# First layer's joined attention maps turned by 16-bit DMA in three head groups, with the second group's product two units later

## The chip, the cores and the metric

The kernel runs on one core of one Trainium2 chip. The metric is the device time of one execution in microseconds. The core has TensorE (PE in the rows; PEld is its weight load), VectorE (DVE), ScalarE (ACT), GpSimd (POOL) and SyncE (SP, which here only issues DMAs). Each engine runs its own list of instructions in order, and semaphores are all that orders one engine against another.

## The reference, cut to what matters

Four transformer layers over 256 tokens of width 1024, all in float32. The first layer's mixer is a differential attention with eight heads, two maps per head, with an ALiBi penalty:

```python
s = jnp.einsum('mbhqd,mbhkd->mbhqk', q, k) * scale + bias    # two maps m = 0, 1 for every head
a = jax.nn.softmax(s, axis=-1)
a = a[0] - lam * a[1]                                       # the joined map
o = jnp.einsum('bhqk,bhkd->bhqd', a, v)                     # 128 columns of v per head
o = rmsnorm(o, subln) * (1.0 - lam_init)
mix = o.reshape(B, S, D_MODEL) @ w_o
```

Each layer goes on with `h = h + mix`, a gated feed-forward block of width 2816, and a gated side input. Layers 2 to 4 have other mixers: neighbourhood, stick-breaking and forgetting attention, 16 heads each.

## The kernel before, in words

**Tiling.** The 256 tokens are T = 2 tiles of 128 query rows. Weights stream from HBM in units of 128x1024 floats through a ring of six buffers. For each unit SyncE loads `raw`, ScalarE writes a rounded copy `whi` (L828), VectorE writes the remainder `wlo` (L1138), and TensorE multiplies in three passes (hi hi, hi lo, lo hi). A layer has 108 units. In the first layer's attention the units 0 to 23 are the QKV projection: four head groups `j` of two heads each, six units per group (four for Q and K, two for V; the V units of two neighbouring groups are shared out over both). Units 24 to 31 are the output projection.

**Order.** Nothing is scheduled at run time. The steps of attention are hung between the units by tables written by hand, `PE_STEPS`, `ACT_STEPS` and `DVE_STEPS`: group `j` has row `r` at unit `6j + 4 + r`. A step stands in front of the engine's work for that unit, or behind it (`+`, or `*` for the groups before the last). ScalarE's work for unit `s` is the split of unit `s+4`, VectorE's the split of unit `s+3`. If two groups have steps at one unit, the later group's come first. The function `steps` (L160) also moves the product steps: `V_WAITS` (L147) gives rows 8, 9 and 10 for `pv0`, `pv1` and `turno`, always behind, and takes the place of the table's rows wherever the line at L172 says so. In the first layer that is for groups 0 and 2. Group 1 keeps the table's rows: `pv0` in front at row 6, `pv1` behind at row 7, `turno` behind at row 8. Group 3, the last, has an order of its own (`last_steps`).

**The steps of a group in the first layer**, tile by tile (0 and 1):
- `evacqk`: Q and K leave PSUM (for groups 1 to 3 VectorE's L1393); `turnqk`: ScalarE's L899 rounds them and VectorE's L1342 writes the remainder `qklo` (named split_qg in the rows).
- `scores0`, `scores1`: TensorE L1818, after both remainders are there; VectorE L1235 takes them from PSUM into `z` with the bias added. Both tiles use the same PSUM banks.
- `exp0`, `exp1`: ScalarE L934.
- `post0`, `post1`: VectorE L1276 to L1282 divides by the sums and joins two maps to one, so that 128x512 floats per tile are left in `z`.
- `turnp0`, `turnp1`: TensorE L1765 transposes the four 128x128 blocks of `z` against the identity into PSUM, and ScalarE L961 copies them to `aT`.
- `pv0`, `pv1`: TensorE L1847 multiplies the turned map by V. ScalarE L966 squares the result for its norm, GpSimd L672 and L673 make `r_o`, the root's inverse, and VectorE L1379 writes the scaled result to `o`.
- `turno`: TensorE L1765 transposes `o`, ScalarE L972 and VectorE L1158 split it into `ohi` and `olo` for the output projection.

**GpSimd** builds the bias of group 3 (`alibi(3)`) and constant tables of later layers (`later_tables`) right after it has made `r_o` of group 1, tile 1. Only then does it come to `r_o` of group 2.

**The other way to turn a map** is there already, for groups 0 to 2 of the second and third layer. VectorE writes the low and the high 16-bit halves of `z` as two planes into the bias tile of the group, which has been used up (`split_p`, L1253); SyncE issues one transposing DMA into `aT` (L553, in `turn_p`); ScalarE puts the halves together again in the bias tile (`join`, L944); the product reads that tile. SyncE waits for the planes of VectorE's step at unit `s-9` just before it loads unit `s`, a load that waits for VectorE's split of the same step.

Of the kernel before, what the change touches and what calls it, by code (L numbers as in the profile page):

```python
# [24 lines left out]
U16 = mybir.dt.uint16  # L25
# [5 lines left out]
P = 128  # L31
S = 256
# [7 lines left out]
HG = 4  # L40
L_DA, L_NA, L_SB, L_FX = range(4)
# [62 lines left out]
def count(labels):  # L104
# [16 lines left out]
    L_FX: [["evacqk"], [], ["turnqk0", "turnqk1/"], ["scores0"], ["scores1"], ["turnp0"], ["turnp1"], ["pvt*"]],  # L121
}
ACT_STEPS = {
    L_DA: [["evacqk"], ["turnqk"], [], ["exp0"], ["exp1"], ["turnp0"], ["pv0", "turnp1"], ["pv1*"], ["turno*"]],
    L_NA: [["evacqk"], ["turnqk"], [], ["exp0"], ["exp1"], ["turnp0"], ["turnp1"], ["pvt*"], ["join0"], ["join1"]],
    L_SB: [["evacqk"], ["turnqk"], [], ["exp0"], ["exp1"], ["turnp0"], ["turnp1"], ["pvt*"], ["join0"], ["join1"]],
    L_FX: [["evacqk"], [], ["turnqk0", "turnqk1+"], [], ["exp0", "exp1+"], ["turnp0"], ["turnp1"], ["pvt*"]],
# [13 lines left out]
def joined(L):  # L141

    return L in (L_NA, L_SB)
# [16 lines left out]
def steps(tables, L, s, place="front"):  # L160

    found = []

    for j in (range(HG) if L == L_FX and s == GROUP_UNITS + QK_UNITS else range(HG)[::-1]):
        r = s - GROUP_UNITS * j - QK_UNITS
        if L == L_FX and j == 0 and r > 0:
            r = r if r == 1 else r - 1 if r > 2 else -1
        if 0 <= r < len(tables[L]) + 3:
            names = tables[L][r] if r < len(tables[L]) else []
            if L == L_DA and j == HG - 1 and r >= LAST_PV:  # L170
                names = last_steps(tables)[r - LAST_PV]
            if j % 2 == 0 or (L == L_FX or joined(L)) and j < HG - 1:  # L172
                names = [x for x in names if x.rstrip("+*") not in V_WAITS[L]]
                names = names + [x + "+" for x in V_WAITS[L] if V_WAITS[L][x] == r]
            for name in names:
                late = name.endswith("+") or name.endswith("*") and j < HG - 1
                if place == ("middle" if name.endswith("/") else "behind" if late else "front"):
                    found.append((name.rstrip("+*/"), j))
    return found


def keys(L, t):
    return P if L >= L_SB and t == 0 else S
# [26 lines left out]

def by_dma(L, j):

    return L in (L_NA, L_SB) and j < HG - 1


P_TURN = count([(L, j, t) for L in range(LAYERS) for j in range(HG) for t in range(T) if by_dma(L, j)])
# [53 lines left out]
EV = {x: n for n, x in enumerate(EV_LIST)}  # L270
# [41 lines left out]
def build(nc, a, out):  # L312
    ctx = ExitStack()
    with ctx:
# [12 lines left out]
        h = sb("h", [P, T, D])  # L327
# [14 lines left out]
        aT, gain = aT_gain[:, 0:T * 1024].rearrange("p (t c) -> p t c", t=T), aT_gain[:, T * 1024:T * 1024 + GAIN_ROWS]  # L342
        bias = sb("bias", [P, T, HG, 1024])
# [52 lines left out]
        tb = [ps(f"turn{b}", [P, 512]) for b in range(2)]  # L396
# [53 lines left out]
        def wait_out(eng, e):  # L450

            eng.wait_ge(turn_out[e % 2], e // 2 + 1)

        def p_source(L, j, t):

            return bias[:, t, j, :].bitcast(U16)[:, 0:8 * keys(L, t)]

        def p_target(L, t):

            return aT[:, t, :].bitcast(U16)[:, 0:8 * keys(L, t)]  # L460

        def p_halves(tile, L, t, h):

            return tile.bitcast(U16).rearrange("p (x c h) -> p x c h", c=S, h=2)[:, :, 0:keys(L, t), h]

        def scores_wait(eng, L, j, t):

# [341 lines left out]
        def _(act):  # L809
# [52 lines left out]
            def attention(L, name, j):  # L862
                t = int(name[-1]) if name[-1] in "01" else 0
# [56 lines left out]
                elif name.startswith("exp"):  # L920
                    if L == L_SB:
                        scores_wait(act, L, j, t)
                        if j and by_dma(L, j - 1):
                            act.wait_ge(p_joined, P_TURN[(L, j - 1, t)])
                        tmp = aT[:, t, :].rearrange("p (x c) -> p x c", c=S)[:, :, 0:kk]
                        act.activation(tmp, zt, ACT.Sigmoid, scale=-1.0)
                        act.activation(zt, zt, ACT.Sigmoid).then_inc(sp_ready, 1)
                    else:
                        if L == L_FX:
                            act.wait_ge(mx_ready, 2 * j + t + 1)  # L930
                        else:
                            scores_wait(act, L, j, t)
                        for x in range(4):
                            ins = act.activation(zt[:, x, :], zt[:, x, :], ACT.Exp, bias=mx[:, t, x:x + 1],  # L934
                                                 scale=-1.0, accum_out=sums[:, t, x:x + 1])
                        ins.then_inc(e_ready, 1)
                elif name.startswith("join"):
                    if not by_dma(L, j):
                        return
                    n = P_TURN[(L, j, t)]  # L940
                    act.wait_ge(p_turned[t], 16 * ((n - 1) // T + 1))
                    for h in range(2):
                        c = 4 * kk
                        ins = act.activation(p_halves(bias[:, t, j, :], L, t, h),  # L944
                                             p_target(L, t)[:, h * c:(h + 1) * c].rearrange("p (x c) -> p x c", c=kk),
                                             ACT.Copy)
                    ins.then_inc(p_joined, 1)
                elif name.startswith("turnp"):
                    if by_dma(L, j):
                        return  # L950
                    e = EV[("p", L, j, t, 0)]
                    act.wait_ge(turned, e + 1)
                    if j and by_dma(L, j - 1):
                        act.wait_ge(p_joined, P_TURN[(L, j - 1, t)])
                    dst = aT[:, t, 0:512]
                    if kk == P:
                        dst = aT[:, t, :].rearrange("p (x k c) -> p x k c", k=2, c=P)[:, :, 0, :]
                        act.activation(dst, tb[e % 2][:, :].rearrange("p (x c) -> p x c", c=P), ACT.Copy)\
                            .then_inc(turn_out[e % 2], 1)
                    else:  # L960
                        act.activation(dst, tb[e % 2][:, :], ACT.Copy).then_inc(turn_out[e % 2], 1)  # L961
                elif name in ("pv0", "pv1"):
                    e = EV[("pv", L, j, t)]
                    act.wait_ge(turned, e + 1)
                    for x in range(2):
                        ins = act.activation(aT[:, t, x * P:(x + 1) * P], tb[e % 2][:, x * P:(x + 1) * P], ACT.Square,  # L966
                                             accum_out=ss_o[:, t, x:x + 1])
                    ins.then_inc(so_ready, 1)
                elif name in ("turno", "pvt"):
                    e = EV[("o", L, j)]  # L970
                    act.wait_ge(turned, e + 1)
                    act.activation(ohi[:, 2 * j:2 * j + 2, :], tb[e % 2][:, :].rearrange("p (k c) -> p k c", k=2),  # L972
                                   ACT.Copy).then_inc(turn_hi, 1)
# [148 lines left out]
        def _(dve):  # L1122
# [125 lines left out]
            def split_p(L, j, t):  # L1248

                for h in range(2):  # L1250
                    c = 4 * keys(L, t)
                    to = p_source(L, j, t)[:, h * c:(h + 1) * c].rearrange("p (x c) -> p x c", x=4)
                    ins = dve.tensor_copy(to, p_halves(z[:, t, :], L, t, h))  # L1253
                ins.then_inc(p_planes, 1)

            def after_exp(L, j, t):
# [20 lines left out]
                if L == L_DA:  # L1277
                    link(dve.tensor_scalar(lamc[:, t, :], rsum[:, t, 2:4], lam[:, 1:2], None, ALU.mult))
                    for b in range(2):
                        e0, e1 = (z[:, t, q * 512 + b * 256:q * 512 + b * 256 + 256] for q in range(2))  # L1280
                        link(dve.tensor_scalar(e1, e1, lamc[:, t, b:b + 1], None, ALU.mult))
                        ins = dve.scalar_tensor_tensor(out=e0, in0=e0, scalar=rsum[:, t, b:b + 1], in1=e1,  # L1282
                                                       op0=ALU.mult, op1=ALU.add)
                    ins.then_inc(a_ready, 1)
                    return
                zt = z[:, t, :].rearrange("p (x c) -> p x c", c=S)[:, :, 0:kk]
                dve.tensor_tensor(zt, zt, rsum[:, t, :].unsqueeze(2).to_broadcast([P, 4, kk]), ALU.mult)\
# [305 lines left out]
        def _(pe):  # L1593
# [182 lines left out]
            def attention(L, name, j):  # L1776
# [62 lines left out]
                elif name in ("pv0", "pv1"):  # L1839
                    e = EV[("pv", L, j, t)]  # L1840
                    use(e)
                    wait_out(pe, EV[("p", L, j, t, 0)])
                    for kt in range(T):
                        pe.wait_ge(bank_out[2 + kt], outs(2 + kt, L, j) + 1)
                    for n, (q, b, k) in enumerate(p_blocks(L, t)):
                        c = b * P
                        ins = pe.matmul(tb[e % 2][:, c:c + P], aT[:, t, n * P:(n + 1) * P],  # L1847
                                        qkv[:, B, k, 512 + c:512 + c + P], start=(k == 0), stop=(k == T - 1))
                    ins.then_inc(turned, 1)
                elif name == "pvt":  # L1850
# [194 lines left out]
```

## Time and profile before

| | |
|---|---|
| median of 3 runs | 1318.11 us (1317.69 to 1318.17) |
| profiled execution | 1318.08 us, of which the span is 1316.0 us |
| TensorE busy | 1300.7 us (99%), 6642 matmuls |
| VectorE busy | 965.8 us (73%) |
| ScalarE busy | 847.4 us (64%) |
| GpSimd busy | 127.5 us (10%) |
| share of the chain that ended last | PE 88%, DVE 7%, ACT 2% |
| granted TensorE clock | 1.000 (2.4 GHz) |

The profile is of one execution; its times are counted from the start of the span. The first layer's attention lies from 0 to about 125 us. Busy shares are means over the whole span, so the stretches have to be read one by one. In a timeline a row is a start, a duration, the engine, the line, the operation, `out<-in`, the size, and how many such instructions the row merges; a bracket at its end tells how long the engine had been idle and who released it. Instructions of one engine overlap a little: the next one starts some hundredths before the last one's end, and with matmuls a tenth or more.

### The profile page before, as it was taken

What the parts mean: (1) busy time and instruction counts of PE and PEld (TensorE: products, weight loads), DVE (VectorE), ACT (ScalarE), POOL (GpSimd) and SP (SyncE); (2) the same over time, 40 slices, a digit from 0 to 9 for tenths busy, and PEclk for the clock granted to TensorE, in tenths of its full rate; (3) what the DMA queues carried; (4) which work ended last, traced back from release to release, by engine and by line L of the source; (5) the groups of instructions that cost most, each with busy time, mean ns of one, the idle gap of its engine ahead of it and who ended that gap; (6) DMA issues with size and microseconds to landing.
All of it is one profiled execution on the core that took longest, in us unless ns stands there. A gap on an engine that the chain in (4) does not pass through costs nothing.

```text
span 1316.0 us, 20045 instructions
## 1 busy us (share of the span) xinstructions
PE 1300.7 (99%) x6642; PEld 1082.7 (82%) x6642; DVE 965.8 (73%) x1669; ACT 847.4 (64%) x1459; POOL 127.5 (10%) x179
## 2 busy tenths in 40 slices
PE   9999999999999999999999999999999999999998
PEld 7987888888898788888888878888887778888887
DVE  7887677777799666666699976666677887666664
ACT  7666666656778666665677666666578766666654
POOL 6031244310000000000010000000002210000000
PEclk9999999999999999999999999999999999999999
DMA  9444688876496466667647656666645535666661
GB/s 335 145 156 136 200 247 243 241 241 176 177 232 195 147 196 207 207 207 213 214 145 198 179 172 197 207 206 211 211 165 183 176 131 163 200 208 209 210 225 48
DMA packets 205056, 255.28 MB, mean 194 GB/s; under 512 B 72962, under 2 KB 163249, under 8 KB 204992
## 3 DMA queue, kind: packets, MB, share of 16 engines
q1 hardware_dynamic: 201984, 245.42, 59.4%
q0 software_dynamic: 2832, 8.49, 2.9%
q8 instruction: 37, 0.61, 0.2%
q10 hardware_dynamic: 176, 0.54, 0.1%
q14 instruction: 27, 0.22, 0.0%
HBM read 238.33 MB, written 1.13 MB: 182 GB/s over the span
## 4 chain that ended last, share of the span: by engine, by line
PE 88%; DVE 7%; ACT 2%; issue 1%; DMA 1%; POOL 0%; SPq 0%; DVEq 0%; ACTq 0%
PE acc L1604 14%; PE acc L1606 13%; PE acc L1605 13%; PE sc L1604 12%; PE sc L1606 12%; PE sc L1605 12%; PE turn L1765 3%; DVE wlo L1138 2%; PE acc L1715 2%; PE acc L1717 2%; PE acc L1716 2%; PE turn L1867 1%; DVE z L1235 1%; PE sc L1818 1%; ACT whi L828 1%
## 5 line engine op out<-in xcount | busy, mean ns | idle before, releaser
L828 ACT ACTIVATE whi<-raw,aT_gain 128x512 fp32r<-128x512 f32 (+2 forms) x612 | 403.8, 720 | 79.5 <-PE sc L1606 53.5
L1138 DVE SCALAR_TENSOR_TENSOR wlo<-raw,aT_gain,whi 128x512 fp32r<-128x512 f32 (+2 forms) x612 | 431.9, 760 | 28.4 <-ACT whi L828 24.2
L1604 PE MATMUL sc<-whi,xhi 128*128 128x512 f32 x640 | 249.4, 390 | 0.0
L1606 PE MATMUL sc<-whi,xlo 128*128 128x512 f32 x640 | 249.0, 389 | 0.0
L1605 PE MATMUL sc<-wlo,xhi 128*128 128x512 f32 x640 | 249.0, 389 | 0.0
L1604 PE MATMUL acc<-whi,xhi 128*128 128x512 f32 x432 | 173.1, 401 | 1.1 <-DVE wlo L1138 0.5
L1606 PE MATMUL acc<-whi,xlo 128*128 128x512 f32 x432 | 168.6, 390 | 0.0
L1605 PE MATMUL acc<-wlo,xhi 128*128 128x512 f32 x432 | 168.4, 390 | 0.0
L828 ACT ACTIVATE whi<-raw 128x1024 fp32r<-128x1024 f32 x120 | 125.9, 1055 | 63.5 <-PE acc L1606 56.9
L1136 DVE TENSOR_TENSOR wlo<-raw,whi 128x1024 fp32r<-128x1024 f32 x120 | 146.5, 1253 | 0.5 <-ACT whi L828 0.5
L1606 PEld LDWEIGHTS sc<-whi,xlo 128*128 128x128 f32 x640 | 120.1, 188 | 25.2
L1604 PEld LDWEIGHTS sc<-whi,xhi 128*128 128x128 f32 x640 | 120.1, 188 | 24.8
L1605 PEld LDWEIGHTS sc<-wlo,xhi 128*128 128x128 f32 x640 | 120.2, 188 | 24.7
L1401 DVE SCALAR_TENSOR_TENSOR aT_gain<-sc,rstd,aT_gain 128x256 f32<-128x256 f32 x80 | 38.7, 483 | 115.0 <-ACT aT_gain L977 115.0
L977 ACT ACTIVATE aT_gain<-sc,rstd 128x256 f32<-128x256 f32 x80 | 38.0, 475 | 127.3 <-PE sc L1606 127.3
L1604 PE MATMUL acc<-whi,split_qg 128*128 128x512 f32 x288 | 112.4, 390 | 0.0
L1606 PE MATMUL acc<-whi,split_qg 128*128 128x512 f32 x288 | 112.1, 389 | 0.0
L1605 PE MATMUL acc<-wlo,split_qg 128*128 128x512 f32 x288 | 112.0, 389 | 0.0
L1604 PEld LDWEIGHTS acc<-whi,xhi 128*128 128x128 f32 x432 | 81.3, 188 | 18.8 <-issue 2.1
L1606 PEld LDWEIGHTS acc<-whi,xlo 128*128 128x128 f32 x432 | 81.1, 188 | 17.5
L1605 PEld LDWEIGHTS acc<-wlo,xhi 128*128 128x128 f32 x432 | 81.4, 189 | 15.1
L672 POOL TENSOR_SCALAR rstd<-ss 128x2 f32<-128x2 f32 x12 | 2.6, 219 | 919.2 <-ACT spare L851 919.2
(212 smaller groups left out, 2068.4 us busy)
## 6 DMA issues: line engine op xcount, KB each, us to landing
raw<-in_ffn_w_gu SPq DMA_DIRECT2D x176, 256.0 KB
raw<-in_qk SPq DMA_DIRECT2D x62, 512.0 KB
raw<-in_ffn_w_gate SPq DMA_DIRECT2D x88, 256.0 KB
raw<-in_ffn_w_up SPq DMA_DIRECT2D x88, 256.0 KB
raw<-in_ffn_w_down SPq DMA_DIRECT2D x44, 512.0 KB
raw<-in_ffn_w_d SPq DMA_DIRECT2D x44, 512.0 KB
raw<-in_ple_w_gate SPq DMA_DIRECT2D x32, 512.0 KB
raw<-in_da_w_qkv SPq DMA_DIRECT2D x8, 512.0 KB
```

The source lines that it names most:

```text
L828: ins = act.activation(whi[:, u % RING, c0:c1], raw[:, u % RING, c0:c1], ACT.Copy, scale=scale)
L977: act.activation(aT[:, 0, t * 256:t * 256 + 256], bank[:, 0:256], ACT.Sigmoid, scale=rs(L, 1, t))\
L1136: ins = dve.tensor_tensor(lo, w, hi.bitcast(F32), ALU.subtract)
L1138: ins = dve.scalar_tensor_tensor(out=lo, in0=w, scalar=gain[:, g:g + 1], in1=hi.bitcast(F32), op0=ALU.mult, op1=ALU.subtract)
L1401: dve.scalar_tensor_tensor(out=sg, in0=banks[t][:, 256:512], scalar=rs(L, 1, t), in1=sg, op0=ALU.mult, op1=ALU.mult).then_inc(gmid, 1)
L1604: pe.matmul(dst, xh, wh, start=first, stop=False)
L1605: pe.matmul(dst, xh, wl, start=False, stop=False)
L1606: return pe.matmul(dst, xl, wh, start=False, stop=last)
L1715: pe.matmul(dst, wh, xh, start=first and k == 0 and c == 0, stop=False)
L1716: pe.matmul(dst, wl, xh, start=False, stop=False)
L1717: ins = pe.matmul(dst, wh, xl, start=False, stop=last and k == 1 and c == 1)
L1765: ins = pe.transpose(tb[e % 2][0:cols, n * rows:(n + 1) * rows], src, ident[0:rows, 0:rows])
```

## The change

Four things are different. First, `by_dma` takes in the first layer, so the maps of its groups 0, 1 and 2 are turned by the DMA instead of TensorE. The helpers get a factor, `p_maps`: two joined maps instead of four, so 128x512 floats per tile, as two planes of 512 16-bit elements. Second, ScalarE gets the steps `join0` and `join1` at rows 7 and 8 of the first layer. Third, the condition in `steps` becomes `j < HG - 1`: group 1 of the first layer now has its product at rows 8 and 9 and its `turno` at row 10, all behind, as the groups 0 and 2 have. For all other layers and groups the condition gives what it gave before. Fourth, TensorE's `pv0` and `pv1` wait for the joined map and read it from the bias tile. Group 3 still has its maps turned by TensorE.

```diff
 ACT_STEPS = {
-    L_DA: [["evacqk"], ["turnqk"], [], ["exp0"], ["exp1"], ["turnp0"], ["pv0", "turnp1"], ["pv1*"], ["turno*"]],
+    L_DA: [["evacqk"], ["turnqk"], [], ["exp0"], ["exp1"], ["turnp0"], ["pv0", "turnp1"], ["pv1*", "join0"],
+           ["turno*", "join1"]],
...
-            if j % 2 == 0 or (L == L_FX or joined(L)) and j < HG - 1:
+            if j < HG - 1:
                 names = [x for x in names if x.rstrip("+*") not in V_WAITS[L]]
...
 def by_dma(L, j):
 
-    return L in (L_NA, L_SB) and j < HG - 1
+    return L in (L_DA, L_NA, L_SB,) and j < HG - 1
...
+        def p_maps(L):
+
+            return 2 if L == L_DA else 4
+
         def p_source(L, j, t):
 
-            return bias[:, t, j, :].bitcast(U16)[:, 0:8 * keys(L, t)]
+            return bias[:, t, j, :].bitcast(U16)[:, 0:2 * p_maps(L) * keys(L, t)]
...
                     ins.then_inc(a_ready, 1)
+                    if by_dma(L, j):
+                        dve.wait_ge(a_ready, 2 * j + t + 1)
+                        split_p(L, j, t)
                     return
...
                 elif name in ("pv0", "pv1"):
                     e = EV[("pv", L, j, t)]
                     use(e)
-                    wait_out(pe, EV[("p", L, j, t, 0)])
+                    if by_dma(L, j):
+                        pe.wait_ge(p_joined, P_TURN[(L, j, t)])
+                    else:
+                        wait_out(pe, EV[("p", L, j, t, 0)])
+                    p_t = bias[:, t, j, :] if by_dma(L, j) else aT[:, t, :]
...
-                        ins = pe.matmul(tb[e % 2][:, c:c + P], aT[:, t, n * P:(n + 1) * P],
+                        ins = pe.matmul(tb[e % 2][:, c:c + P], p_t[:, n * P:(n + 1) * P],
```

`p_target`, `p_halves`, `split_p` and the join take `p_maps(L)` in place of 4 in the same way.

## Rows read from the trace of the kernel before

**Rows 1.** The page, part 1: busy us, share of the span, instructions.
```profile
PE 1300.7 (99%) x6642; PEld 1082.7 (82%) x6642; DVE 965.8 (73%) x1669; ACT 847.4 (64%) x1459; POOL 127.5 (10%) x179
```

**Rows 2.** Table by stretch: length, busy per engine, clock, DMA share, GB/s.
```profile
28.50:50.80 22.30, 22.12 (x171) 20.44 (x170) 21.91 (x61) 13.83 (x34) 1.49 (x4) 1.00 0.60 194
58.53:72.00 13.47, 12.51 (x85) 11.32 (x84) 13.15 (x31) 9.18 (x23) 1.06 (x2) 1.00 0.44 150
77.37:96.42 19.05, 19.05 (x132) 17.04 (x131) 18.77 (x45) 12.74 (x29) 6.37 (x16) 1.00 0.52 172
```

**Rows 3.** Chain of waits: start, us, what; one set of four transposes.
```profile
37.83 0.44 PE turn L1765 x4
```

**Rows 4.** Timeline of TensorE in the first layer.
```profile
46.98 0.39 PE L1818 MATMUL sc<-qkT 64*128 64x256 f32 x2
...
55.73 1.05 PE L1847 MATMUL turn<-qkv,aT_gain 128*128 128x128 f32 x8
...
61.05 0.66 PE L1765 MATMUL turn<-ident,z 128*128 128x128 f32 x4 [0.96 <-DVE z L1282]
...
71.24 1.05 PE L1847 MATMUL turn<-qkv,aT_gain 128*128 128x128 f32 x8
72.22 0.39 PE L1818 MATMUL sc<-qkT 64*128 64x256 f32 x2
...
76.10 0.60 PE L1765 MATMUL turn<-ident,o 128*128 128x128 f32 x4
...
92.71 0.38 PE L1818 MATMUL sc<-qkT 64*128 64x256 f32 x2
```

**Rows 5.** Timeline of VectorE in the first layer.
```profile
44.08 1.43 DVE L1342 TENSOR_TENSOR split_qg<-qkv,qkT 128x256 fp32r<-128x256 f32 x4
...
58.53 0.42 DVE L1379 TENSOR_TENSOR o<-turn,r_o 128x256 f32<-128x256 f32 x1 [1.71 <-POOL r_o L673]
...
60.51 0.48 DVE L1282 SCALAR_TENSOR_TENSOR z<-z,rsum 128x256 f32<-128x256 f32 x1
60.91 1.41 DVE L1138 SCALAR_TENSOR_TENSOR wlo<-raw,aT_gain,whi 128x512 fp32r<-128x512 f32 x2
...
69.32 1.42 DVE L1342 TENSOR_TENSOR split_qg<-qkv,qkT 128x256 fp32r<-128x256 f32 x4
...
77.37 0.69 DVE L1158 TENSOR_TENSOR olo<-turn,ohi 128x512 fp32r<-128x512 f32 x1
...
80.68 0.17 DVE L1276 RECIPROCAL rsum<-sums 128x4 f32<-128x4 f32 x1
...
89.89 1.42 DVE L1342 TENSOR_TENSOR split_qg<-qkv,qkT 128x256 fp32r<-128x256 f32 x4
```

**Rows 6.** Timeline of VectorE in the third layer: planes of a tile of 128x512.
```profile
687.49 0.69 DVE L1269 TENSOR_TENSOR z<-z,aT_gain 128x508 f32<-128x508 f32 x1
688.21 0.76 DVE L1253 COPY bias<-z 128x512 uint16<-128x512 uint16 x2
```

**Rows 7.** Timeline of TensorE in the second layer.
```profile
396.78 0.39 PE L1818 MATMUL sc<-qkT 64*128 64x256 f32 x2 [1.28 <-DVE split_qg L1338]
```

**Rows 8.** Timeline of VectorE in the second layer, just before rows 7.
```profile
395.01 1.67 DVE L1338 SCALAR_TENSOR_TENSOR split_qg<-qkv,lam_in,qkT 128x256 fp32r<-128x256 f32 x4
```

**Rows 9.** The transposing DMAs' line: issue ns min/median/max; then time to landing.
```profile
L553 SPq DMA_TRANSPOSE aT_gain<-bias x12: 1237/1835/3716, 365.0 to 733.2; - x12
...
DMA to landing us min/median/max: 3.3/4.3/6.6
```

**Rows 10.** Timeline of ScalarE in the third layer: the join of a tile of 128x512.
```profile
695.76 1.40 ACT L944 ACTIVATE bias<-aT_gain 128x512 uint16<-128x512 uint16 x2
```

**Rows 11.** Timeline of GpSimd in the first layer: bias of group 3, end of the tables.
```profile
74.09 4.41 POOL L666 TENSOR_SCALAR bias<-nab 128x256 f32<-128x256 f32 x8
...
88.17 0.22 POOL L737 TENSOR_SCALAR_AFFINE_SELECT window<-window 64x48 f32<-64x48 f32 x1
```

**Rows 12.** Timeline of VectorE beside GpSimd's first bias builds.
```profile
19.78 3.16 DVE L1138 SCALAR_TENSOR_TENSOR wlo<-raw,aT_gain,whi 128x512 fp32r<-128x512 f32 x4 [1.22 <-ACT whi L828]
```

## Prediction: what the change does to the time

> **Bound now.** The page's busy times come first: TensorE (PE) is busy 99% of the span and VectorE (DVE) 73% [rows 1]. Read alone, that says a PE cut comes out whole and DVE work is free. The table by stretch says otherwise for the layer that is changed: DVE works 21.91 of 22.30 us from 28.50 on, 13.15 of 13.47 from 58.53, and 18.77 of 19.05 from 77.37 [rows 2]. Between these stretches it waits for r_o, the norm of the product (PE product, ScalarE squares, GpSimd power, then DVE's o). So in this layer DVE has no cover of its own except in those waits.
>
> Units are numbered by PE: group j has its first QK unit at 6j, unit 6j+4+r is its row r in the step tables. scores0 of group j+1 (units 12, 18, 24) needs DVE's qk_lo (L1342) of the unit before. Before the change PE starts these at 46.98, 72.22 and 92.71 [rows 4], and L1342 ends at 44.08+1.43 = 45.51, 69.32+1.42 = 70.74 and 89.89+1.42 = 91.31 [rows 5]: slacks of 1.47, 1.48 and 1.40 us. How thin that is shows in the second layer, which turns by DMA already: there PE sat 1.28 us before scores for qk_lo [rows 7], and started 396.78-(395.01+1.67) = 0.10 us after L1338 ended [rows 8].
>
> **What PE loses.** Six sets of four transposes at 0.44 us each in the chain of waits [rows 3]: 2.64 us. The set of group 1, tile 0, also waited 0.96 us for z [rows 4]; nobody waits there now. Together 3.6 us: what a PE-bound reading gives. The deferral moves two products by two units each; it removes nothing. A product costs 72.22-71.24 = 0.98 us [rows 4].
>
> **What DVE gets.** Per tile, a wait for its own z and two copies of 128x512 16-bit elements. The third layer's tile 0 has exactly this shape: the pair takes 0.76 us and starts 0.03 us after its source ends at 687.49+0.69 [rows 6]. Instructions that don't wait start some 0.08 us before the last one ends (60.51+0.48 against 60.91, [rows 5]); the pair gives that back at its end and loses it at its start. So 0.76+0.03 = 0.79, taken as 0.80 us per tile, 1.6 us per group. Nothing is taken off DVE: the evictions that go were ScalarE's. It cannot be below zero; the upper bound, half again for other strides, is 1.2 per tile.
>
> **The chain, step by step.**
> Group 0: DVE works without a break from post0 to qk_lo of group 1, so L1342 ends at 45.51+1.6 = 47.11, and scores0 of group 1 starts at 47.2 instead of 46.98. PE, 0.88 us early by its two lost sets, would have been there at 46.1; it waits 1.1 us, and the gain is gone: +0.2 against before. DVE's wait for r_o that follows (o starts 58.53-55.73 = 2.80 us after its product, [rows 4, 5]) takes the rest of DVE's delay.
> Group 1: before, from o at 58.53 to the end of L1342 at 70.74 are 12.2 us [rows 5]. Added: 1.6; gone: the o of product 0, 0.42-0.08 = 0.34. So 13.5. The product of tile 1 of group 0 starts at 55.73+0.2 = 55.95, o at 58.75, L1342 ends at 72.2, scores0 of group 2 starts at 72.3. PE would be ready at 72.22+0.2-1.96-0.88-0.96 = 68.6: it sits 3.7 us. It starts the scores when it did before, but with the two products (1.96 us) still to do.
> Group 2: products and scores alternate now: scores0 at 72.3, product 0 after 76.10-72.22 = 3.88, scores1 after 0.98, product 1 after another 3.88, at 81.1; o at 83.9. Only then does DVE come to post0 of group 2, which began at 80.68 before [rows 5]. From there to the end of L1342 at 91.31 were 10.6 us; added are o itself (0.34), the olo of the moved turno (0.69-0.08 = 0.6, [rows 5], which lay ahead of post0 before) and 1.6: 13.2. L1342 ends at 97.0, scores0 of group 3 starts at 97.1 instead of 92.71: **+4.4**. PE would be ready at 72.3+(92.71-72.22)+1.96-0.88 = 93.9 and sits 3.2 us.
> After that nothing gives it back or adds to it: DVE waits for r_o of group 2 again, and the last group keeps its own order and its PE transposes. All later weight loads are paced by units.
>
> **What lies beside.** ScalarE loses six evictions and gets twelve copies, 1.40 us for a pair of this shape [rows 10]; it sat in waits for PE, and its joins lie ahead of splits four units early: no cost, up to 0.7 us if a join delays an exp. SP gets six transposing DMAs; its wait for the planes lies ahead of a load that waits for DVE's split of the same step anyway. Issuing takes it 1.2 to 3.7 us and landing 3.3 to 6.6 [rows 9]; the loads queued behind have some five units until they are split, so nothing. The least time from planes to join is about 5 us (group 2, tile 1: planes at 92, join at 97). Even a landing at 6.6 delays ScalarE by some 1.6 us, which splits four units ahead cover.
> GpSimd: the last bias and the tables start after group 1's product 1, so at 84 instead of 74.09; they took until 88.4 [rows 11], 14.3 us, and end near 98.3. r_o of group 2 is due at about 102.7 and the bias at 98: both in time, by 4 and 10 us. But the bias build (4.41 us) now lies beside post0 and the copies of group 2. Four splits beside GpSimd's first bias took 3.16 us [rows 12], where two pairs at 1.41 less overlaps make 2.74 [rows 5]: 15% more. On 4.2 us of DVE that is at most 0.6; zero if these forms are not touched; I take 0.2.
> The Trainium skill has a rule for this (SBUF — State Buffer, SBUF: two separate sides): VectorE and GpSimd share a port pair that one of them holds for a whole instruction while the other blocks. The slower splits agree with it.
>
> **Sum.** 4.4+0.2 = +4.6 us on the profiled run's 1318.08 (span 1316.0 and 2.1 around it), which stands within 0.1 of the median 1318.11: 1322.7 us, a span of 1320.6. The copies at 1.2 per tile would add 0.8 in group 1's chain and 0.8 in group 2's, and GpSimd 0.4 more than taken: up to 1324.7. If the two waits for r_o come out half a microsecond shorter each (2.30 for 2.80): 1321.7.
>
> The Trainium skill says to transpose a full 128x128 block on TensorE if a PSUM destination is acceptable, and by DMA otherwise (VectorE: DVE Perf Modes, Rules for kernel authors). It speaks against this change, for another reason than mine; by that rule alone one would expect a loss here too, and no row tells its size.
>
> **Rivals.**
> 1. **PE keeps what it is relieved of** (faster). It decides if DVE's extra work per group stays under the slack of 1.47 us less what PE comes early, 0.6 us in group 0. [rows 1] speak for it; [rows 2, 6, 7] against. Time: 1318.1-3.6 = 1314.5. Chance 0.10.
> 2. **The first long wait doesn't form** (no change). If group 1's chain were 3.7 us shorter, scores0 of group 2 would start at 68.6, product 1 at 77.4, and group 3's scores at 93.4 instead of 92.71: 1318.8. It needs a DVE that works the stretch from 58.53 with less than its steps take, though it was busy for 13.15 of 13.47 us: chance 0.10.
> 3. **The clock falls.** PE sits 3.7 and 3.2 us, against 0.96 and 1.28 in the waits shown [rows 4, 7], and the granted clock was 1.00 in every stretch of [rows 2]. If it went to the lower of its levels after such a wait, the 3.88 us from scores0 to the next step would take up to twice as long; this is in series with the forecast: +2 to +4 for one fall, 1324.7 to 1326.7. Nothing in the rows shows a fall: chance 0.08.
> The Trainium skill warns of just this: long idle gaps between matmul bursts bring TensorE back to half clock (TensorE: Matmul & The Clock Gate, Why this matters for your kernels).
> 4. **The change doesn't arrive as meant**: the DMA lands so late that joins hold ScalarE, and exp and post with it. If the 1.6 us by which the longest landing of [rows 9] is over the 5 us of group 2 reach DVE's post through one exp: 1324.3. Chance 0.06.
> The forecast has the remaining 0.66.
>
> **Range and chances.** The forecast's own range is 1321.7 to 1324.7. Two in ten outside allow one to leave out rival 1 and most of a fall of the clock, so the range goes from 1318.7 (rival 2, just below) to 1326.2. A measurement of this kernel tells 0.2%, 2.6 us, from no change. Faster by more: rival 1, 0.10. Within: rival 2 and a thin lower edge of the forecast, 0.12. Slower by more: 0.78.
>
> **What would show it.** In the changed kernel's list of waits: PE waits for split_qg L1342 before scores three times, about 1.1, 3.7 and 3.2 us, and no wait for z of group 1. DVE busy over 97% from post0 to L1342 of each group. scores0 of group 3 near 97. In the layers behind, all steps later by the same amount. POOL's tables end near 98. The granted clock 1.00 throughout. Wrong it would be made by waits under 1 us at these places (rival 1 or 2), by PE waiting for the joined planes (rival 4), or by DVE copies far from 0.8 us per tile.

## The result and the profile after

The changed kernel takes 1326.64 us (median; 1325.81 to 1327.69), the kernel before 1318.09 beside it: a ratio of 1.0066 with a 95% interval of 1.0054 to 1.0078, +8.5 us. The forecast was 1322.7 in a range of 1318.7 to 1326.2, so the sign was right and the size was not: +8.5 for +4.6, just over the upper end. The profiled execution is the longest of those shown, 1327.69 us with a span of 1325.9 (+9.9 on 1316.0).

The list of waits of the changed kernel (engine, line, what it waited for: us in total, times, longest). L1826 are the scores, L1350 is qk_lo (L1342 before), L1773 the transposes on PE:

```profile
PE sc L1826 <- DVE split_qg L1350: 8.9, 3, 4.2
...
PE turn L1773 <- DVE z L1287: 1.5, 2, 1.1
```

Three waits, as forecast, and none of PE for a joined plane. The steps of PE around them, from its timeline (start us, us, line, operation, tiles, [idle before, what ended it]); L1859 is the product with the values:

```profile
46.76 0.39 PE L1826 MATMUL sc<-qkT 64*128 64x256 f32 x2 [0.95 <-DVE split_qg L1350]
...
71.87 0.58 PE L1826 MATMUL sc<-qkT 64*128 64x256 f32 x2 [3.67 <-DVE split_qg L1350]
72.22 0.45 PE L1826 MATMUL sc<-split_qg,qkT 64*128 64x256 f32 x2
...
78.28 0.28 PE L1724 MATMUL acc<-xhi,wlo 128*128 128x256 f32 x1
...
78.52 1.05 PE L1859 MATMUL turn<-qkv,bias 128*128 128x128 f32 x8
...
83.37 1.05 PE L1859 MATMUL turn<-qkv,bias 128*128 128x128 f32 x8
100.32 0.58 PE L1826 MATMUL sc<-qkT 64*128 64x256 f32 x2 [4.24 <-DVE split_qg L1350]
...
106.44 1.05 PE L1859 MATMUL turn<-qkv,bias 128*128 128x128 f32 x8
```

Starts in two traces can be compared to some 0.4 us only. The scores of group 0 are ahead of everything that the change touches. The first line here has them in the kernel before, the second in the changed kernel; the third is, in the kernel before, the product that starts at 106.44 above:

```profile
26.68 0.39 PE L1818 MATMUL sc<-qkT 64*128 64x256 f32 x2 [0.26 <-DVE split_qg L1158]
...
26.31 0.38 PE L1826 MATMUL sc<-qkT 64*128 64x256 f32 x2 [0.26 <-DVE split_qg L1163]
...
96.51 1.05 PE L1847 MATMUL turn<-qkv,aT_gain 128*128 128x128 f32 x8
```

Counted from scores0 of group 0, scores0 of group 1 comes after 20.45 us for 20.30 before (+0.15), and scores0 of group 2 after 45.56 for 45.54.

Up to 71.87 this is the forecast: 0.95 for 1.1, 3.67 for 3.7, a start at 71.87 for 72.3. Then comes what it did not have. The product follows 6.65 us after these scores (78.52-71.87) instead of 3.88 [rows 4], and between them one scores matmul takes 0.45 us, where the others show 0.28 to 0.31. The table by stretch, with stretches chosen at such steps (span of the stretch; PE, PEld, DVE, ACT, POOL busy; granted clock; DMA share; GB/s):

```profile
55.00:68.00 13.00, 13.00 (x90) 11.89 (x88) 10.91 (x29) 7.40 (x20) 0.88 (x2) 1.00 0.42 104
71.87:78.00 6.13, 6.13 (x33) 5.91 (x34) 4.02 (x12) 2.94 (x5) 0.00 (x0) 0.50 0.56 173
78.50:99.00 20.50, 17.58 (x130) 16.02 (x128) 15.60 (x36) 12.00 (x36) 9.63 (x23) 0.99 0.40 101
100.32:105.50 5.18, 5.18 (x21) 4.18 (x22) 4.98 (x12) 2.58 (x4) 0.00 (x0) 0.50 0.60 199
106.50:120.00 13.50, 12.32 (x73) 9.96 (x71) 8.72 (x25) 9.37 (x29) 1.79 (x4) 1.00 0.32 99
```

After each of the two long waits the granted clock was 0.50, the lower of its two levels (1.2 GHz for 2.4), for the next 6.2 and 5.2 us, in which PE worked without a break. The Trainium skill names this (TensorE: Matmul & The Clock Gate, Why this matters for your kernels): long idle gaps between bursts of matmuls bring the engine back to half clock. The trace agrees for these two, at 3.67 and 4.24 us.

A further departure is on DVE. Its steps after the o of group 1 (L1387), with the z operations of post0 (L1286, L1287) and the copies (L1258):

```profile
86.17 0.42 DVE L1387 TENSOR_TENSOR o<-turn,r_o 128x256 f32<-128x256 f32 x1 [1.73 <-POOL r_o L678]
...
86.72 0.40 DVE L1283 TENSOR_SCALAR lamc<-rsum,lam 128x2 f32<-128x2 f32 x1
87.15 0.55 DVE L1286 TENSOR_SCALAR z<-z,lamc 128x256 f32<-128x256 f32 x1
87.74 0.56 DVE L1287 SCALAR_TENSOR_TENSOR z<-z,rsum 128x256 f32<-128x256 f32 x1
...
89.34 1.05 DVE L1258 COPY bias<-z 128x512 uint16<-128x512 uint16 x2
...
92.46 0.23 DVE L1283 TENSOR_SCALAR lamc<-rsum,lam 128x2 f32<-128x2 f32 x1
...
93.11 0.48 DVE L1287 SCALAR_TENSOR_TENSOR z<-z,rsum 128x256 f32<-128x256 f32 x1
93.51 0.35 DVE L1286 TENSOR_SCALAR z<-z,lamc 128x256 f32<-128x256 f32 x1
93.90 0.48 DVE L1287 SCALAR_TENSOR_TENSOR z<-z,rsum 128x256 f32<-128x256 f32 x1
94.42 0.76 DVE L1258 COPY bias<-z 128x512 uint16<-128x512 uint16 x2
```

and GpSimd in the same time:

```profile
86.22 3.88 POOL L671 TENSOR_SCALAR bias<-nab 128x256 f32<-128x256 f32 x8
```

The same operations take 0.40, 0.55, 0.56 and 1.05 us beside the bias build, and 0.23, 0.35, 0.48 and 0.76 six microseconds later. From L1283 to the end of the copies that makes 3.67 us for 2.72, 0.95 more. What lies behind adds nothing: the product of group 2 already starts 9.93 us later than before (106.44 for 96.51), the whole of the 9.9 us between the spans.

### The profile page after: what moved, and what is told of

It reads as the page before. It is cut to its first block, busy times and chain, and to the rows that moved or that the text cites. A ratio compares the mean times of both kernels' runs of the same rounds, so it can differ in the third digit from the quotient of the medians.

```text
span 1325.9 us, 20022 instructions
## 1 busy us (share of the span) xinstructions
PE 1302.6 (98%) x6618; PEld 1084.2 (82%) x6618; DVE 970.8 (73%) x1681; ACT 852.0 (64%) x1465; POOL 126.0 (10%) x179
## 4 chain that ended last, share of the span: by engine, by line
PE 85%; DVE 10%; ACT 2%; issue 1%; DMA 1%; POOL 0%; SPq 0%; DVEq 0%; ACTq 0%
PE acc L1612 13%; PE acc L1614 13%; PE acc L1613 13%; PE sc L1612 12%; PE sc L1614 11%; PE sc L1613 11%; DVE wlo L1143 3%; PE turn L1773 3%; PE acc L1723 2%; PE acc L1724 2%; PE acc L1725 2%; PE turn L1879 1%; DVE z L1240 1%; PE sc L1826 1%; DVE z L1287 1%
```

## The experiments

All times are medians, with the kernel before beside them at 1317.80 to 1318.00. The chain theory says: DVE's work from o to qk_lo of groups 1 and 2 sets when PE gets its next scores; the copies and the moved product lengthen it. The rivals were a fall of the clock and GpSimd's work beside DVE.

**One part alone: the copies.** The kernel before, with this behind post of groups 0 to 2 (nobody reads the copies; PE still transposes):

```
+ if j < HG - 1:
+     dve.wait_ge(a_ready, 2 * j + t + 1)
+     for h in range(2):
+         dve.tensor_copy(<plane h>, <half h of z>)
```

> The kernel before, with VectorE's two 16-bit copies added to each tile of groups 0 to 2 and nothing else: TensorE still turns the maps, the planes are used by nobody. Theory (VectorE's chain to qk_lo decides): each group's 1.6 us eat the slack of 1.4 to 1.5 us before scores; TensorE waits for split_qg before scores three times, each under 1 us, the clock stays at 1.00, and the kernel is 0.7 to 1.2 us slower than before. Rival (the copies are the whole cost): 5 to 8.5 us slower. Rival (the DMA or the deferral is the cost): no change.

Measured 1319.12 us, ratio 1.0011 (1.0001 to 1.0021): +1.3. The size holds, near enough; the place does not. PE waited for z before its transposes, 3.1 us in five waits (2.5 in three before), and not for qk_lo. A likely reason, argued and not tested: while PE transposes it has its own work to put against DVE's 1.6 us a group, and what is over shows at the next thing that it needs from DVE.

**One part alone: the deferral.**

```
-            if j % 2 == 0 or (L == L_FX or joined(L)) and j < HG - 1:
+            if j < HG - 1:
```

> The kernel before, with group 1's two products two units later and turno too, TensorE still turning all maps. Theory: VectorE now reaches post0 of group 2 only after the second product's o, and qk_lo of group 3 ends near 93.6 instead of 91.3 while TensorE wants it at 92.9: 1 us slower than before, clock 1.00, one wait for split_qg of about 0.8 us. Rival (deferral is harmless): no change within 0.2 us. Rival (deferral is most of the loss): 4 us and more.

Measured 1321.69, 1.0029 (1.0017 to 1.0040): +3.8 for an expected +1. PE's waits in that kernel:

```profile
PE turn L1765 <- DVE z L1282: 5.7, 6, 1.6
```

The product that is moved takes its o with it, and that o now stands ahead of post0 of group 2 on DVE. So post0 waits for PE's product, ScalarE's squares and GpSimd's norm, and what PE needs next (here z for its transposes, in the changed kernel qk_lo) comes late. The bias build of GpSimd moves too, since it follows the last r_o of group 1, and lies beside that post0:

```profile
82.55 4.14 POOL L666 TENSOR_SCALAR bias<-nab 128x256 f32<-128x256 f32 x8
...
83.47 0.56 DVE L1281 TENSOR_SCALAR z<-z,lamc 128x256 f32<-128x256 f32 x1
...
85.55 1.68 DVE L1138 SCALAR_TENSOR_TENSOR wlo<-raw,aT_gain,whi 128x512 fp32r<-128x512 f32 x2
```

From L1278 to the end of that pair of splits the trace has 4.19 us, where the same steps of group 1 in the changed kernel without its copies take 3.25: some 0.9 of the 3.8 us are an estimate of GpSimd's part.

**The change without its copies.** The copies of L1258 are left out of the changed kernel, so that what is transposed for groups 0 to 2 is not the map.

> The changed kernel without the twelve copies on VectorE: the DMA turns whatever the bias tiles hold, so the first layer's maps of groups 0 to 2 are wrong, and everything else runs as in the changed kernel. Theory: TensorE waits for split_qg about 0, 2.1 and 2 us before the three scores instead of 0.95, 3.67 and 4.24; the clock stays at 1.00; 1 to 2 us slower than before, 6.5 to 7.5 faster than the changed kernel. Rival (DMA, joins on ScalarE or the port are the cost): within 1.5 us of the changed kernel's 1326.6.

Measured 1320.37, 1.0021 (1.0012 to 1.0031): +2.5, over the 1 to 2 expected with a steady clock. The waits are near the expected ones, 2.10 and 2.54 us. Single runs lie between 1319.04 at a mean clock of 1.000 and 1323.41 at 0.996, so the time goes with the clock. In the profiled run it fell after the shorter of the two waits:

```profile
60.00:80.00 20.00, 17.90 (x124) 16.24 (x123) 15.61 (x44) 13.00 (x32) 0.89 (x2) 0.91 0.58 158
```

So the copies are not a small part. Without them 6.0 of the 8.55 us are gone, and the one run at clock 1.000 is 1.2 us slower than before, just the +3.8 of the deferral less 2.64 us for the six sets of transposes [rows 3]. Alone the copies cost 1.3 us; in the changed kernel, beside the deferral and without PE's transposes, far more.

**Without the fall of the clock.** The changed kernel with dummy matmuls in the long waits of groups 2 and 3 (called filler below):

```
+ if L == L_DA and j >= 2 and t == 0:
+     pe.wait_ge(z_ready, ATT[(L, j, t)] - 1)
+     spin(13)
```

> The changed kernel with 13 idle matmuls of the identity (some 2.9 us) ahead of TensorE's wait for qk_lo in groups 2 and 3, where it waited 3.67 and 4.24 us. They add work to nothing that is late. Theory (the clock fell after those two waits, which cost the rest): the mean granted clock is back at 1.000, the waits for split_qg shrink to about 1 us, and the kernel takes 1322.5 to 1323.5, 3 to 4 us less than the changed kernel. Rival (the clock is not the cause, all of it is the chain): 1326 to 1327 as before.

Measured 1323.29, 1.0042 (1.0025 to 1.0059). What PE then shows, the dummies on L1916:

```profile
68.19 3.06 PE L1916 MATMUL sc<-ident 128*128 128x128 f32 x26
72.03 0.39 PE L1829 MATMUL sc<-qkT 64*128 64x256 f32 x2 [0.77 <-DVE split_qg L1350]
...
97.72 0.39 PE L1829 MATMUL sc<-qkT 64*128 64x256 f32 x2 [1.34 <-DVE split_qg L1350]
```

The scores start at 72.03 as without them (71.87), the next matmuls take 0.31 us, and the granted clock is 1.00 where it was 0.50:

```profile
72.03:78.00 5.97, 5.97 (x57) 5.58 (x58) 3.94 (x12) 3.97 (x11) 0.21 (x2) 1.00 0.65 208
97.72:103.00 5.28, 5.28 (x40) 4.53 (x42) 4.98 (x12) 3.03 (x8) 0.00 (x0) 1.00 0.59 186
```

PE does dozens of small matmuls more, 26 in this wait alone, and the kernel is 3.35 us faster (1326.64-1323.29; 3.1 if each is taken against the kernel before beside it). That is what the clock took.

**Where the chain decides, and from where on.** Only groups 0 and 2 turned by DMA, group 1 as before, with no deferral:

> The changed kernel with group 1 as before the change: its maps are turned by TensorE and its product stands at rows 6 and 7. Groups 0 and 2 are turned by DMA. Theory: the copies of group 0 cost the 0.95 us wait and no more; group 1 runs as before; qk_lo of group 3 ends near 92.7, 1.2 us after TensorE could use it. 1318.0 to 1318.8, clock 1.00, the losses of the full change (8.5 us) nearly all gone. Rival (each group's DMA turn costs its share): two thirds of the loss, 1323 to 1324.

Measured 1317.85, 1.0002 (0.9992 to 1.0011). PE has lost four sets of transposes, 1.76 us by [rows 3], and waits for qk_lo instead, 2.0 us in two waits (0.93 and 1.05). By the medians that is an even trade, a little below the expected 1318.0 to 1318.8.

**The deferral halved.** Group 1's products one unit later instead of two:

> The changed kernel with group 1's products and turno one unit later than before instead of two (rows 7, 8 and 9, behind). VectorE then meets the second product's o before scores1 of group 2 and not after it, so post0 of group 2 isn't behind a wait. Theory: the wait before scores0 of group 2 is 2.7 us instead of 3.67, scores0 of group 3 comes near 95.3 with the clock up instead of 97.7 (kernel filler); 2.5 us from the chain and 1.3 to 3 from clock falls: 1322 to 1324, at least 2 us below the changed kernel. Rival (where the product stands doesn't matter, only the copies do): 1326 to 1327.

Measured 1321.84, 1.0037 (1.0022 to 1.0052), and again with the clock: 1320.60 and 1320.71 at 1.000, 1321.84 and 1321.87 at 0.998, 1326.03 at 0.994. One kernel, 5.4 us apart. The wait of group 1 is another one than expected. The product now stands ahead of scores0 of group 2, and PE sat 3.08 us before it. The profile names no releaser, but ScalarE's join (L950) of this map ended at 71.45, 0.1 us before:

```profile
70.07 1.38 ACT L950 ACTIVATE bias<-aT_gain 128x512 uint16<-128x512 uint16 x2
...
71.55 1.13 PE L1860 MATMUL turn<-qkv,bias 128*128 128x128 f32 x8 [3.08 <-issue]
```

The join stood behind ScalarE's rounding of Q and K, which waited for DVE's L1402, so DVE is in this chain too. Qk_lo itself was there at 72.05, and the scores started at 72.61. In this run the clock held through the wait of 3.08 us:

```profile
71.50:77.00 5.50, 5.45 (x49) 5.23 (x50) 4.45 (x15) 4.22 (x10) 0.88 (x2) 1.00 0.61 191
```

**The copies twice**, with the dummies of filler:

> The kernel filler with every copy done twice (the second pair goes to an unused part of the bias tile): 0.68 us more of VectorE per tile, 1.36 per group. Theory (no slack is left in any of the three chains): all of it comes out, 3 x 1.36 = 4.1 us more than filler, 1327.4; where the waits now outlast the idle matmuls by 2 us the clock may fall and add up to 3. Rival (VectorE's waits for r_o take part of it): less than 2 us more, 1325 at most.

Measured 1330.07, 1.0096 (1.0079 to 1.0113): 6.8 us over filler. Counted from scores0 of group 0 (26.13 here, 26.46 in filler), scores0 of the groups 1, 2 and 3 comes 1.33, 2.67 and 4.16 us later than in filler: each of the three chains grew by what was added to it, as expected. The rest is the clock: the last wait grew to 2.83 us in spite of the dummies ahead of it, from 100 to 120 the granted clock was 0.83, against 1.00 in filler, and the product came 6.63 us after scores0 of group 3 for 3.76.

**GpSimd's share, first try.** Filler with the last bias built after group 0's product, at 59, instead of after group 1's:

> The kernel filler with GpSimd's bias build for group 3 right after group 0's product instead of group 1's, so it no longer runs beside post0 and the copies of group 2. Theory (the port they share slowed these, 2.1 us for post0's four passes by the changed kernel's rows where before had them faster): the four passes and the copies are back at their durations, scores0 of group 3 comes 0.8 to 1.0 us earlier, and the kernel takes 1322.3 to 1322.6. Rival (the slower rows are not GpSimd's): the same 1323.3 as filler.

Measured 1324.23, 1.0045 (1.0028 to 1.0061), no gain. The bias build had found the other chain, that from the o of group 0:

```profile
60.02 0.56 DVE L1287 TENSOR_SCALAR z<-z,lamc 128x256 f32<-128x256 f32 x1
60.61 0.56 DVE L1288 SCALAR_TENSOR_TENSOR z<-z,rsum 128x256 f32<-128x256 f32 x1
```

From scores0 of group 1 to that of group 2 this kernel takes 26.07 us, filler 25.12; from there to group 3 24.71, filler 25.69. What was won in group 2 was lost in group 1.

**GpSimd's share, second try.** The bias where DVE has slack of its own:

```
+ if t == 0 and j == 0:
+     pool.wait_ge(unit_done, 12)
+     alibi(3)
```

> The kernel of the run filler (the changed kernel with spinning matmuls before the long waits) with one edit: GpSimd builds the last bias right after unit 12 has begun, at about 47, where VectorE waits 1.46 us for r_o a little later and so has slack of its own. No part of the chains from o to qk_lo of groups 1 and 2 then lies beside GpSimd's bias. My theory: post0 of group 2 is back at 0.35 and 0.48 us an operation, the copies at 0.8 a pair, and the time is what the VectorE chain alone gives: 1323.3 less 0.9 = 1322.4 (1322.0 to 1322.8), scores0 of group 3 near 96.8. Rival (the 0.9 us is not GpSimd's, or it moves into the chain of group 1 by a late r_o, as with the early bias): 1323.3 or more.

Measured 1321.90, 1.0031 (1.0020 to 1.0043), 1.4 us faster than filler by the medians, a little more than expected. Their spans are 1.0 apart (1321.1 and 1320.1), and scores0 of group 3 starts at 96.70, 1.02 earlier. DVE in group 2:

```profile
85.61 0.48 DVE L1289 SCALAR_TENSOR_TENSOR z<-z,rsum 128x256 f32<-128x256 f32 x1
86.13 0.76 DVE L1260 COPY bias<-z 128x512 uint16<-128x512 uint16 x2
```

What is left, 1321.90 against 1318.00, is the chain with neither the clock's fall nor the bias build in it: **+3.9**.

**The planes made by GpSimd.** The same copies on the idle engine, with the last bias after group 0's product. First the whole change:

> The changed kernel as it is, but with the planes of the first layer made by GpSimd (last bias after group 0's product, tables after group 2's). If only VectorE's own copies mattered, this is the changed kernel without copies, 1319 to 1320.4, with waits of some 2.1 and 2.5 us for split_qg before scores0 of groups 2 and 3. If GpSimd's copies slow VectorE by a third of a microsecond per tile, it is 1321 to 1322, with waits nearer 3 us and the chance that the granted clock falls after one.

Measured 1323.20, 1.0037 (1.0023 to 1.0051): the worse of the two cases expected, and over its 1322. DVE has no copy left, and PE still waited 3.75 us, as what stands beside GpSimd's work is slow: a pair of DVE's weight splits took 1.68 and 1.76 us where it takes 1.41. The clock fell twice in the profiled run, the second time after a wait of only 1.92 us.

```profile
59.18 0.56 DVE L1300 SCALAR_TENSOR_TENSOR z<-z,rsum 128x256 f32<-128x256 f32 x1
...
65.55 1.76 DVE L1154 SCALAR_TENSOR_TENSOR wlo<-raw,aT_gain,whi 128x512 fp32r<-128x512 f32 x2
...
71.27 0.58 PE L1836 MATMUL sc<-qkT 64*128 64x256 f32 x2 [3.75 <-DVE split_qg L1360]
...
97.17 0.39 PE L1836 MATMUL sc<-qkT 64*128 64x256 f32 x2 [1.92 <-DVE split_qg L1360]
```

```profile
98.00:101.00 3.00, 3.00 (x12) 2.29 (x9) 3.00 (x12) 1.91 (x3) 0.00 (x0) 0.50 1.02 386
```

GpSimd's pairs beside these took longer too:

```profile
61.87 1.50 POOL L788 COPY bias<-z 128x512 uint16<-128x512 uint16 x2
65.69 2.09 POOL L788 COPY bias<-z 128x512 uint16<-128x512 uint16 x2 [2.32 <-DVE z L1300]
```

Then with group 1's products one unit later:

> The changed kernel with the planes of the first layer made by GpSimd, group 1's products one unit later instead of two, the last bias after group 0's product and the rest of the tables after group 2's. All three groups still turn by DMA. My theory: with the copies off VectorE the waits for split_qg shrink below 1.2 us, PE keeps part of its six sets of 0.44 us (2.64 us), and the time is 1316 to 1317.5 at a clock of 1.00. Rival (GpSimd slows VectorE, or the deferral by one unit costs by itself as two units alone cost 3.8 us): 1318.5 to 1321.

Measured 1320.60, 1.0020 (1.0011 to 1.0029), the rival's time. As with the deferral halved, PE waited before the product, here for 3.16 us until a join had ended, and then the clock fell: from 72.5 to 75.5 it was 0.50. And with groups 0 and 2 alone:

> The changed kernel with three edits: the 16-bit planes of the first layer are made by GpSimd instead of VectorE, only groups 0 and 2 turn by DMA (group 1 as in the kernel before), and GpSimd's last bias is built after group 0's product. My theory (VectorE's chain to qk_lo decides and its copies are what lengthens it): VectorE has only its old work, so scores0 of each group starts as early as PE allows. PE loses four sets of four transposes at 0.44 us, 1.76 us: 1316.3, with waits for split_qg under 1 us and scores0 of group 3 near 91. Rival (the planes cost as much wherever they are made, since GpSimd's copies lie beside VectorE's splits and slow them): each of four copy pairs costs VectorE some 0.3 to 0.7 us, and the time is 1317.8 to 1320. A second rival is that GpSimd's copies take so long (over 3 us a pair) that the joined planes are late and PE waits for them: over 1320.

Measured 1317.43 (1317.18 to 1317.85), 0.9997 (0.9988 to 1.0006): no difference by its interval, and 1.1 over the expected 1316.3. PE waited there for z of group 1, whose post0 lay beside the bias build:

```profile
61.07 0.65 PE L1783 MATMUL turn<-ident,z 128*128 128x128 f32 x4 [1.62 <-DVE z L1300]
```

With the bias in the slack after unit 12 as well:

> The kernel of the run gp_02 with the same edit (last bias right after unit 12 has begun). In gp_02 PE waited 1.62 us for z of group 1 at 61.07, 0.96 in the kernel before; the bias lay beside that post0 and made its operations 0.55 us instead of 0.35 and 0.48. My theory: the wait falls to about 1.0, and the time to 1316.6 to 1316.9, faster than the kernel before. Rival (the waits behind take the place): 1317.4, no change against gp_02.

Measured 1316.66 (1316.32 to 1317.21), 0.9989 (0.9980 to 0.9998): the one version clear of noise below the kernel before, by 1.3 us.

```profile
60.39 0.66 PE L1784 MATMUL turn<-ident,z 128*128 128x128 f32 x4 [0.97 <-DVE z L1301]
...
91.19 0.39 PE L1837 MATMUL sc<-qkT 64*128 64x256 f32 x2
```

Counted from scores0 of group 0, scores0 of group 3 comes 1.4 us earlier than before, close to the 1.76 us of PE's four sets. Of the versions run, the relief came through only in this one, where DVE makes no copies, no product is deferred and the bias build is out of the chains.

## Why the prediction was right and wrong

The sum, from three kernels that differ by one thing each: the chain 1321.90-1318.00 = 3.9, GpSimd's work beside it 1323.29-1321.90 = 1.4 (1.0 in the traces), the clock 1326.64-1323.29 = 3.35. They add up to the measured 8.55 but for the 0.1 between the kernels before, as they must, since each is a difference to the next kernel; it is the traces that tell what each one is. The clock's part is 3.1 and GpSimd's 1.5 if each kernel is taken against the one before beside it.

**The chain, forecast +4.4 (of which 0.2 in group 0): +3.9.** Its steps, forecast and found:

| step | forecast | found |
|---|---|---|
| pair of copies | 0.76 | 0.76 (1.05 beside GpSimd) |
| PE's wait, scores0 of group 1 | 1.1 | 0.95 |
| PE's wait, scores0 of group 2 | 3.7 | 3.67 |
| scores0 of group 2 | 72.3 | 71.87 |
| scores0 of group 3 | 97.1 (+4.4) | 96.70 (clock and GpSimd taken out; +4.15 counted from scores0 of group 0), 100.32 in the changed kernel |
| PE's wait there | 3.2 | 4.24 |
| product to o | 2.80 | 2.79 and 2.80 (78.52 to 81.31, 83.37 to 86.17) |

The rule that carried it, that DVE has no cover between two waits for r_o, held best where it was tested alone: with the copies doubled each chain grew by the 1.3 to 1.5 us that were added. What the text said of the parts was less good. It gave the deferral no price of its own ("it removes nothing") and spread it over the terms of group 2 as the o and olo ahead of post0. The run with the deferral alone shows +3.8, some 0.9 of it GpSimd's, with PE's transposes still in place. An estimate from three runs shows how the parts meet while the clock holds: +3.8 for the deferral, -2.6 for the six sets of transposes, +4.2 for the copies (what their doubling added), together +5.4, and filler measured 5.4 over the kernel before. The price of the order was in the sum, under another name.

**The clock, forecast 1.00 throughout: the failed step.** The sum had nothing for a fall of the clock, and it took 3.35 us. Rival 3 had the place (after the waits of 3.7 and 3.2 us) and the size of one fall (+2 to +4; found 6.65-3.88 = 2.8 for the first). It had a chance of 0.08 since no row of before shows a fall. But the waits that those rows show are of 0.96 and 1.28 us [rows 4, 7]: they say nothing about one of 3.7. Nothing in the rows spoke for a stable clock either, and the only evidence at that length, the Trainium skill's rule named beside the rival, spoke for a fall. There were also two long waits and not one, and the runs gave both: 3.35 us in the medians, and 4.8 between the spans of the two profiled runs (1325.9 for 1321.1 in filler); the other three runs of the changed kernel had a higher mean clock (0.995 to 0.997 for 0.994). The second fall shows as the lag from scores0 of group 3 to its product, 106.44-100.32 = 6.12 us, where filler takes 101.48-97.72 = 3.76.

**GpSimd, forecast +0.2 of at most 0.6: +1.0 to 1.4, the mis-sized term.** The overlap was seen in advance, and sized from the wrong row: splits at 15% more [rows 12], applied to post0 and the copies. Those forms suffer far more. From the rows above: L1283 0.40 for 0.23 (74% more), L1286 0.55 for 0.35 (57%), L1287 0.56 for 0.48 (17%), the pair of copies 1.05 for 0.76 (38%). The upper end of 0.6 was therefore no bound. The Trainium skill's rule (SBUF — State Buffer, SBUF: two separate sides) was cited for this and gave no size.

**What lies beside, forecast nothing: right.** In the changed kernel PE never waited for a joined plane. The joins of group 1 ended at 71.2 and 73.6, and the six transfers of the first layer landed 3.1 to 3.6 us after their issue. The joins and SP's six issues cost nothing that shows there. With the product one unit earlier PE did wait until a join had ended (3.08 us): the deferral by two units is what keeps the joins out of the way.

**Rival 1** (PE keeps 3.6 us) fell, but the last version above shows from where on it begins to be true: the copies off DVE, no deferral, GpSimd's other work out of the chains. Of 1.76 us, 1.3 came through. **Rival 2** (the first long wait doesn't form) and **rival 4** (late transfers) did not occur in the changed kernel. The range fell 0.4 us short. It left out "most of a fall of the clock" as one of the two in ten; with the fall at the likelihood that its own wait lengths asked for, it might have reached at least to the 1326.7 that the rival gave for one fall, and held the result. That is argued, from the text of the prediction.

Open: whether a given wait of 1.9 to 3.2 us brings the lower clock. The runs show both, and what decides it in a single run is not seen.

## What to carry to other kernels

Before an engine's work is moved to a "free" one, follow that one between its own waits: an average of 73% busy was 98% where it counted, and the relief of 3.6 us came back as waits. A step that is moved takes the steps that hang on it along; ask in front of whom they now stand in the other queues. And if a forecast holds an idle stretch of TensorE that is longer than any in the trace, put a price on the fall of its clock, since the rows of before can't exclude it.

## What the runs showed of the hardware

Three things were not expected. First, the clock: it falls after waits of TensorE, and the length of the wait alone doesn't say whether.

| wait, us | kernel | granted clock |
|---|---|---|
| 4.24, 3.67 | changed | at 0.50 when PE went on, for 5.2 and 6.2 us |
| 3.75 | the whole change, planes by GpSimd | at 0.50 when PE went on |
| 3.16 | planes by GpSimd, one unit later | fell some 1.7 us after PE went on |
| 3.08, 2.47 | deferral halved | stayed at 1.00 |
| 2.83 | copies twice, dummies ahead | at 0.50 when PE went on |
| 2.54 | no copies | stayed at 1.00 |
| 2.28 | copies twice, group 1, no dummies | stayed at 1.00 |
| 2.10 | no copies | fell some 0.9 us after PE went on |
| 1.92 | the whole change, planes by GpSimd | fell some 0.4 us after PE went on |

Dummy matmuls of 3.06 us in the waits of the changed kernel kept it at 1.00.

Second, DVE beside GpSimd: operations of 0.23 to 0.76 us took 17 to 74% longer beside the bias build, and a pair of weight splits 1.76 for 1.41 beside GpSimd's copies. Third, GpSimd isn't a cheap place for the copies: a pair took it 1.50 to 2.16 us beside a working DVE, where DVE does it in 0.76.
